# Four raw buffers and a longer lead for a stream of weight blocks in a two-layer encoder kernel

## Chip, cores and metric

The kernel runs on one core of a Trainium2 chip. The metric is the device time of one execution in microseconds (us), the median of several runs.

## What is computed

Two layers, each with an attention mixer and a PEER feed-forward part, on 512 tokens of width 1024, all in float32. The change touches the second part only:

```python
def peer_ffn(x, w_q, sub_keys, u, v):
    ...
        q = (xc @ w_q).reshape(c, PEER_HEADS, 2, PEER_HALF_DIM)
        sc = jnp.einsum('chpd,hpnd->chpn', q, sub_keys, preferred_element_type=jnp.float32)
        top_s, top_i = lax.top_k(sc, kk)
        cand = top_s[:, :, 0, :, None] + top_s[:, :, 1, None, :]
        cand_s, cand_i = lax.top_k(cand.reshape(c, PEER_HEADS, kk * kk), kk)
        ...
        experts = i1 * PEER_N_KEYS + i2
        gates = jax.nn.softmax(cand_s, axis=-1)
        ue = jnp.take(u, experts, axis=0)
        ve = jnp.take(v, experts, axis=0)
        act = jax.nn.gelu(jnp.einsum('chkd,cd->chk', ue, xc), approximate=False)
        return jnp.einsum('chk,chkd->cd', gates.astype(xc.dtype) * act, ve)
```

There are 8 heads, 16 experts per head and token, and 16384 experts of one neuron each. Around it, `x <- LayerNorm(alpha * x + peer)`.

## The kernel before

**Two ways to the same sum.** For the last 384 of the 512 tokens the kernel computes all experts densely: it streams u and v in 128 blocks of 128 experts each (512 KB a block), multiplies, applies gelu and weights the result with gates that are mostly zero. For the first 128 tokens it gathers the rows of u and v that were chosen and forms 128 row products per token on VectorE.

**Stages of a layer.** Projections and attention (to about 385 us in layer 1); the query stage, 16 blocks of `peer_w_q` and the key scores (to about 495); the expert stage, 128 blocks of u; the value stage, 128 blocks of v (1205 to 1725). Layer 2 repeats this some 1730 us later. The expert stage has two parts. In the first, TensorE takes blocks 0 to 88 while VectorE finds the top 16 (32 "units" of 128 tokens and one head; 8 before the gathers and 24 beside them) and forms 96 row products in 12 rounds of two units and eight rows. At its end VectorE and ScalarE turn the scores into gates, and TensorE transposes them before block 89. In the second part one-hot matrices spread the gates over the experts, beside the other blocks.

**A block's way.** A block of the stream passes through these hands, numbered n over the whole layer, with s = n mod 2:

- SyncE's queue asks for it: `st_load` (L378 to L381) waits until the raw buffer is free, then transfers 512 KB into `st_raw[s]`.
- ScalarE rounds it to fp32r: `round_block` (L848 to L852) waits for the landing and until TensorE has used block n-2 (`st_used`), then copies `st_raw` to `st_hi[s]`.
- GpSimd takes the rest: `rest_block` (L605 to L610) writes `st_lo[s] = st_raw[s] - st_hi[s]` and increments `st_l[s]`. For the blocks of v after the first two VectorE does it (`rest_value`, L1379 to L1384), and for query block 0 too.
- TensorE multiplies: `stationary` (L1626 to L1637) waits for `st_h`, makes 16 products with `st_hi` (L1632, L1633), waits for `st_l` and makes 8 with `st_lo` (L1636). In the value stage it is `gather` and `part` (L1715).

The buffers `st_raw`, `st_hi` and `st_lo` have two places each. `st_raw[s]` is free again when `rest_block` has read it, so a block's load waits for the subtraction of the block two before it. The semaphore starts at 1 in each slot:

```python
            def st_load(m, s, src):
                sp.wait_ge(st_l[s], ST_PER // 2 * l + m + 1)
                sp.dma_start(st_raw[:, s], src).then_inc(s_straw[s], 16)
```

**Orders written out by hand.** Every engine executes its list in order. SyncE's queue alternates, in the expert stage, the store of a gelu result (`gelu_store`, L394 to L397: 192 KB from `h_out[s]` to DRAM, after `gelu_done`) and the load of the block of u four further on. In the value stage it alternates a load of v with `gated_load` (L399 to L403), which brings gates and gelu values back. Before the third block of v it waits for the last one-hot product (`g_tok`) and for all gelu stores. ScalarE alternates, for each block b of the expert stage, `gelu(b)` (L877 to L882; it waits for TensorE to finish b and for the store of b-2 to land) and `round_block(b+2)`, with a table load before each pair. After the pair of blocks 86 and 87 (and the rounding of 88 and 89) comes the exponential of the gates (L904), whose sum VectorE takes in L1312; L1316 finishes the gates.

GpSimd alternates subtractions and gathers. `zone` (L634 to L643) fixes the pattern: in `ZONE_R` = 4 rounds of 8 gathers it places `ZONE_BN` = 26 subtractions evenly, after `ZONE_B0` = 6 at the start. A gather (`gather_rows`, L617 to L621; 512 KB into one of 8 places of `u_row`) waits until VectorE has used that place's row of the round before (`u_dot`). VectorE's row products (L1287) stand inside the units, and wait for the gathered row.

**Memory.** The attention part and the PEER part share the same addresses. After `st_raw`, `st_hi`, `st_lo` and `h_out` come `keys` and `pq`, then `scores`, all in the place of the attention's projections, and behind them the top-16 tables and the index tables. In its loop over the four groups of output weights (`k == 2`, L384) the queue waits until nearly all of attention's inputs are read (`v_ready`), then loads `keys` and the first two query blocks, ahead of the last two blocks of the output projection's weights (`w_load`, L359 to L362).

Of the kernel before, what the change touches and what calls it, by code (L numbers as in the profile page):

```python
# [32 lines left out]
P = 128  # L33
L = 2
T = 512
# [47 lines left out]
ZONE_R, ZONE_B0, ZONE_BN = 4, 6, 26  # L83
# [50 lines left out]
def build(nc, a, out):  # L134
# [56 lines left out]
    o_all = att.tile("o_all", [P, TB, JOBS * VD], F32)  # L191
    w_uq = att.tile("w_uq", [P, 2, UQ_W], F32)
# [34 lines left out]
    st_raw = pr.tile("st_raw", [P, 2, DC * P], F32)  # L227
# [4 lines left out]
    keys = pr.tile("keys", [P, QB, NK], F32)  # L232
    pq = pr.tile("pq", [P, 2, T], F32)
# [10 lines left out]
    cab = tk.tile("cab", [P, 2, TOPK], U32)  # L244
    c_all = tk.tile("c_all", [P, UNITS, TOPK], F32)
# [4 lines left out]
    sp_r = Region(tk.end)  # L250
# [31 lines left out]
    assert max(vp.end, sp_r.end) <= ga.start and vp.end <= tk.end and vr.end <= ln_rows_at and tk.end <= u_at  # L282
# [14 lines left out]
    s_straw = [sem(f"s_straw{s}") for s in range(2)]  # L297
# [52 lines left out]
    def _(sp):  # L350
        for dst, src in ((x_tok[:], a["x"]), (ident[:], a["ident"]), (iota[:], a["iota"])):
            sp.dma_start(dst, src).then_inc(s_x, 16)
        with sp.Fori(0, L) as l:
# [24 lines left out]
            def st_load(m, s, src):  # L378

                sp.wait_ge(st_l[s], ST_PER // 2 * l + m + 1)  # L380
                sp.dma_start(st_raw[:, s], src).then_inc(s_straw[s], 16)  # L381

            for k in range(O_G):
                if k == 2:  # L384


                    sp.wait_ge(v_ready, (JOBS - JA) * (l + 1))
                    sp.dma_start(ln_rows[:], a["ln1"][l].partition_broadcast(P)).then_inc(s_ln, 16)
                    sp.dma_start(keys[:], a["peer_keys"][l]).then_inc(s_keys, 16)
                    for s in range(2):  # L390
                        st_load(0, s, a["peer_w_q"][l, s])
# [13 lines left out]
            with sp.Fori(1, QB // 2) as i:  # L405
                for s in range(2):
                    st_load(i, s, a["peer_w_q"][l, 2 * i + s])
# [25 lines left out]
            st_load(1 + (QB + EB) // 2, 0, a["peer_v"][l, 2])  # L433
            for s in range(2):
                gated_load(1, s)
            st_load(1 + (QB + EB) // 2, 1, a["peer_v"][l, 3])
            gated_load(2, 0)
            with sp.Fori(2, EB // 2 - 1) as i:
                for s in range(2):
                    st_load(i + (QB + EB) // 2, s, a["peer_v"][l, 2 * i + s])  # L440
                    gated_load(i + s, 1 - s)
            st_load(EB // 2 - 1 + (QB + EB) // 2, 0, a["peer_v"][l, EB - 2])
            gated_load(EB // 2 - 1, 1)
            st_load(EB // 2 - 1 + (QB + EB) // 2, 1, a["peer_v"][l, EB - 1])
# [7 lines left out]
    def _(pool):  # L452
        step = Steps(pool, pool_step)
        pool.sem_inc(st_l[1], 1)
# [6 lines left out]
        with pool.Fori(0, L) as l:  # L461
# [150 lines left out]
            rest_block(0, 1)  # L612
            with pool.Fori(1, QB // 2 + ZONE_B0 // 2) as m:
                for s in range(2):
                    rest_block(m, s)
# [19 lines left out]
            def zone(z, first=False):  # L635

                done = 0
                for r in range(ZONE_R):
                    for k in round_u(ZONE_R * z + r, r % 2, first and r == 0):
                        while done * ZONE_R * URING < (URING * r + k + 1) * ZONE_BN - ZONE_BN // 2:  # L640
                            rest_block(z * (ZONE_BN // 2) + QB // 2 + (ZONE_B0 + done) // 2, done % 2)
# [1157 lines left out]
```

## Time and profile before

| | us |
|---|---|
| median of 3 runs (lowest, highest) | 3488.45 (3486.89, 3492.88) |
| the profiled execution | 3488.86 |
| its span | 3487.1 |
| TensorE busy | 3273.4 (94%) |
| VectorE busy | 2486.1 (71%) |
| ScalarE busy | 1371.2 (39%) |
| GpSimd busy | 1955.6 (56%) |
| moved by transfers | 765.12 MB, mean 219 GB/s |

The span runs from the first to the last instruction of the profiled execution; its own time is 1.8 us longer. Busy TensorE includes time at a lower granted clock, which the profile gives apart (1.00 is 2.4 GHz). A wait is put down to the instruction that ended it. Waits of engines that are not the last to arrive cost nothing.

### The profile page before, as it was taken

Reading aid. Unit: us, or ns where it says so; the run is one execution under the profiler, and the core shown is the slowest. Engines: PE = TensorE matmul, PEld = TensorE weight load, DVE = VectorE, ACT = ScalarE, POOL = GpSimd, SP = SyncE. Lnnn points to the kernel's source line nnn. Section 1 sums busy time; section 2 is a strip of 40 time slices with the busy share of each in tenths; the row PEclk is TensorE's granted clock in tenths of the full one; section 3 lists DMA queues with packets and bytes.
Section 4 is the critical chain, followed back from the end, with each engine's and each line's share of the span. In section 5 each row is a group of like instructions: output and inputs, shape, how many; then the busy total and the mean of one; then the engine's idle time right before and its main releaser. Section 6 shows DMA issues by size and latency. Waiting matters only on the chain.

```text
span 3487.1 us, 67389 instructions
## 1 busy us (share of the span) xinstructions
PE 3273.4 (94%) x18454; PEld 2957.4 (85%) x18454; DVE 2486.1 (71%) x5419; ACT 1371.2 (39%) x2110; POOL 1955.6 (56%) x1558
## 2 busy tenths in 40 slices
PE   8999899998999899999899998989999998999996
PEld 8888789988999788888798887889999997788885
DVE  1454557887687688888914545578887777889888
ACT  2354234544433333333324542444444333333332
POOL 3434347877654266666544343477775533666665
PEclk9999999999999999999999999999999999999998
DMA  4001138888698599999820011389886986999996
GB/s 161 25 1 61 43 104 280 296 284 277 223 271 254 165 328 342 336 338 336 306 95 24 1 61 49 121 278 312 285 294 223 275 230 199 315 345 337 339 336 229
DMA packets 402487, 765.12 MB, mean 219 GB/s; under 512 B 162400, under 2 KB 261472, under 8 KB 398432
## 3 DMA queue, kind: packets, MB, share of 16 engines
q1 hardware_dynamic: 197088, 462.06, 39.4%
q0 software_dynamic: 73728, 268.47, 21.0%
q10 hardware_dynamic: 131584, 33.56, 4.6%
q8 instruction: 40, 0.66, 0.1%
q14 instruction: 47, 0.39, 0.0%
HBM read 677.98 MB, written 85.98 MB: 219 GB/s over the span
## 4 chain that ended last, share of the span: by engine, by line
PE 57%; issue 20%; POOL 11%; DVE 3%; ACTq 3%; DMA 3%; ACT 2%; POOLq 1%; DVEq 0%; SPq 0%
PE ps L1715 25%; POOL st_lo L608 6%; PE ps L1682 4%; PE ps L1568 3%; POOL u_row L619 3%; PE ps L1632 3%; PE ps L1633 3%; PE ps L1446 3%; PE ps L1636 3%; PE ps L1447 3%; PE ps L1448 3%; PE ps L1545 3%; ACTq L929 2%; PE ps L1553 2%; PE ps L1534 1%
## 5 line engine op out<-in xcount | busy, mean ns | idle before, releaser
L608 POOL TENSOR_TENSOR st_lo<-st_raw,st_hi 128x1024 fp32r<-128x1024 f32 x290 | 697.2, 2405 | 590.8 <-ACT st_hi L852 585.9
L852 ACT CAST st_hi<-st_raw 128x1024 fp32r<-128x1024 f32 x544 | 571.1, 1050 | 908.8 <-PE ps L1715 444.7
L1632 PE MATMUL ps<-t_hi,st_hi 128*128 128x384 f32 (+1 forms) x2304 | 815.9, 354 | 58.0 <-ACT st_hi L852 56.4
L1633 PE MATMUL ps<-t_lo,st_hi 128*128 128x384 f32 (+1 forms) x2304 | 801.4, 348 | 0.0
L712 POOL TENSOR_TENSOR wt_lo<-w_f,wt_hi 128x384 fp32r<-128x384 f32 x256 | 416.8, 1628 | 319.2 <-ACT wt_hi L954 316.1
L1632 PEld LDWEIGHTS ps<-t_hi,st_hi 128*128 128x128 f32 x2304 | 440.3, 191 | 84.0 <-ACT st_hi L852 68.1
L1636 PE MATMUL ps<-t_hi,st_lo 128*128 128x384 f32 (+1 forms) x2304 | 468.4, 345 | 2.2 <-POOL st_lo L608 2.1
L1633 PEld LDWEIGHTS ps<-t_lo,st_hi 128*128 128x128 f32 x2304 | 440.5, 191 | 10.0
L1636 PEld LDWEIGHTS ps<-t_hi,st_lo 128*128 128x128 f32 x2304 | 412.7, 189 | 16.3 <-POOL st_lo L608 5.1
L1715 PE MATMUL ps<-st_hi,wt_hi 128*128 128x512 f32 x1536 | 391.0, 390 | 9.9 <-ACT wt_hi L954 9.9
L1715 PE MATMUL ps<-st_lo,wt_hi 128*128 128x512 f32 x1536 | 389.8, 389 | 0.0
L1715 PE MATMUL ps<-st_hi,wt_lo 128*128 128x512 f32 x1536 | 389.7, 389 | 0.0
L1382 DVE TENSOR_TENSOR st_lo<-st_raw,st_hi 128x1024 fp32r<-128x1024 f32 x252 | 315.0, 1250 | 79.3 <-ACT st_hi L852 78.0
L1715 PEld LDWEIGHTS ps<-st_hi,wt_hi 128*128 128x128 f32 x1536 | 287.5, 188 | 73.2 <-ACT st_hi L852 10.3
L1715 PEld LDWEIGHTS ps<-st_lo,wt_hi 128*128 128x128 f32 x1536 | 288.3, 188 | 60.0
L1715 PEld LDWEIGHTS ps<-st_hi,wt_lo 128*128 128x128 f32 x1536 | 288.3, 188 | 59.9
L1391 DVE SCALAR_TENSOR_TENSOR ps<-v_row,w_sp,ps 128x1024 f32<-128x1024 f32 x256 | 326.9, 1277 | 0.8
L1374 DVE TENSOR_TENSOR w_f<-g_in,h_in 128x256 f32<-128x256 f32 x256 | 252.2, 985 | 61.9 <-DMA h_in<-gelu_d 48.0
L1287 DVE CUSTOM_DVE_ANT_0 u_row<-ps,u_row 128x1024 f32<-128x1024 f32 x192 | 233.1, 1214 | 84.8 <-DMA u_row<-in_peer_ur,idx_u 83.6
L882 ACT ACTIVATE h_out<-ps 128x384 f32<-128x384 f32 x256 | 125.2, 489 | 425.0 <-PE ps L1636 371.7
L619 POOL DMA_INDIRECT v_row<-in_peer_v,idx_v x256 | 257.5, 1006 | 44.5 <-issue 18.4
L1338 DVE TENSOR_SCALAR oh<-ps,i_t,g_t 128x128 f32<-128x128 f32 x768 | 260.5, 400 | 0.0
(194 smaller groups left out, 5091.7 us busy)
## 6 DMA issues: line engine op xcount, KB each, us to landing
st_raw<-in_peer_u SPq DMA_DIRECT2D x256, 512.0 KB
st_raw<-in_peer_v SPq DMA_DIRECT2D x256, 512.0 KB
gelu_d<-h_out SPq DMA_DIRECT2D x256, 192.0 KB
h_in<-gelu_d SPq DMA_DIRECT2D x256, 192.0 KB
gates_d<-g_stage ACTq DMA_DIRECT2D x32, 1024.0 KB
g_in<-gates_d SPq DMA_DIRECT2D x256, 128.0 KB
w_raw<-in_w_in SPq DMA_DIRECT2D x16, 1168.0 KB, 5.2
st_raw<-in_peer_w_q SPq DMA_DIRECT2D x32, 512.0 KB
```

Of the source, the lines that this page charges most:

```text
L608: nc.gpsimd.tensor_tensor(st_lo[:, s].rearrange("p c f -> p (c f)"), st_raw[:, s], st_hi[:, s].rearrange("p c f -> p (c f)").bitcast(F32), ...
L619: nc.gpsimd.indirect_dma_start(out=dst, out_offset=None, in_=table, in_offset=bass.IndirectOffsetOnAxis(ap=number, axis=0)).then_inc(lande ...
L712: nc.gpsimd.tensor_tensor(wt_lo[:, s], w_f[:, s], wt_hi[:, s].bitcast(F32), ALU.subtract).then_inc(wt_l, 1)
L852: nc.scalar.copy(st_hi[:, s].rearrange("p c f -> p (c f)"), st_raw[:, s]).then_inc(st_h, 1)
L1338: last = nc.vector.tensor_scalar(oh_1[:, GRP * r + k], iota_ps, i_t[:, 0, ds(t0 + k, 1)], g_t[:, ds(t0 + k, 1)], ALU.is_equal, ALU.mult)
L1374: nc.vector.tensor_tensor(w_f[:, s, 0:T_D], g_in[:, s], h_in[:, s, 0:T_D], ALU.mult)
L1382: nc.vector.tensor_tensor(st_lo[:, s].rearrange("p c f -> p (c f)"), st_raw[:, s], st_hi[:, s].rearrange("p c f -> p (c f)").bitcast(F32), ...
L1391: nc.vector.scalar_tensor_tensor(out=acc, in0=v_row[:, r], scalar=w_sp[:, ds(b, 1)], in1=acc, op0=ALU.mult, op1=ALU.add).then_inc(v_acc, 1)
L1632: nc.tensor.matmul(dst, st_hi[:, s, c], t_hi[:, c, rows], start=c == 0, stop=False)
L1633: nc.tensor.matmul(dst, st_hi[:, s, c], t_lo[:, c, rows], start=False, stop=False)
L1636: last = nc.tensor.matmul(dst, st_lo[:, s, c], t_hi[:, c, rows], start=False, stop=c == DC - 1)
L1715: last = nc.tensor.matmul(ps[:, 2 * d + half], w[:, s, d * P:(d + 1) * P], v[:, half * 512:(half + 1) * 512], start=False, stop=True, skip ...
```

## The change

`st_raw` gets four places instead of two (`RAW = 4`), each with its own landing semaphore; `st_hi` and `st_lo` keep two. The semaphores `st_l` start at 2 (`PRIME`), so that a load waits for the subtraction of the block four before it. In the expert stage the load after the gelu store of block b is that of block b+6 instead of b+4; the first four blocks of v are asked for there. In the value stage loads of v stand two blocks further ahead of the gate products. Four query blocks instead of two are asked for before the last weights of the output projection. `keys` and `pq` move to the place of the attention's tables, and the index tables behind the buffers of the value stage. The zones of GpSimd become 6 rounds with 40 subtractions (`ZONE_R`, `ZONE_BN`). Loops over blocks run over four places at once or are unrolled.

```diff
-ZONE_R, ZONE_B0, ZONE_BN = 4, 6, 26
+ZONE_R, ZONE_B0, ZONE_BN = 6, 6, 40
+VALUE_BYTES = 4 * (3 * TN + 2 * OH_T * P + UDOTS * D + 2 * T_D + 8 * TN)
+RAW = 4
...
+    tables_at = att.end
...
-    st_raw = pr.tile("st_raw", [P, 2, DC * P], F32)
+    st_raw = pr.tile("st_raw", [P, RAW, DC * P], F32)
...
-    keys = pr.tile("keys", [P, QB, NK], F32)
-    pq = pr.tile("pq", [P, 2, T], F32)
+    qk = Region(tables_at)
+    keys = qk.tile("keys", [P, QB, NK], F32)
+    pq = qk.tile("pq", [P, 2, T], F32)
...
-    sp_r = Region(tk.end)
+    sp_r = Region(shared + VALUE_BYTES)
...
-            def st_load(m, s, src):
+            def st_load(m, r, src):
-                sp.wait_ge(st_l[s], ST_PER // 2 * l + m + 1)
-                sp.dma_start(st_raw[:, s], src).then_inc(s_straw[s], 16)
+                sp.wait_ge(st_l[r % 2], ST_PER // 2 * l + m + 1)
+                sp.dma_start(st_raw[:, r], src).then_inc(s_straw[r], 16)
...
-                    for s in range(2):
-                        st_load(0, s, a["peer_w_q"][l, s])
+                    for r in range(RAW):
+                        st_load(r // 2, r, a["peer_w_q"][l, r])
...
-            for b in range(4):
-                st_load(QB // 2 + b // 2, b % 2, a["peer_u"][l, b])
-            with sp.Fori(0, EB // 2 - 2) as i:
-                for s in range(2):
-                    gelu_store(i, s)
-                    st_load(i + QB // 2 + 2, s, a["peer_u"][l, 2 * i + 4 + s])
-            for s in range(2):
-                gelu_store(EB // 2 - 2, s)
-                st_load((QB + EB) // 2, s, a["peer_v"][l, s])
+            for b in range(RAW + 2):
+                st_load(QB // 2 + b // 2, b % RAW, a["peer_u"][l, b])
+            with sp.Fori(0, EB // RAW - 2) as i:
+                for r in range(RAW):
+                    gelu_store(2 * i + r // 2, r % 2)
+                    st_load(2 * i + QB // 2 + RAW // 2 + 1 + r // 2, (r + 2) % RAW, a["peer_u"][l, RAW * i + RAW + 2 + r])
+            for b in range(EB - 2 * RAW, EB - 2):
+                gelu_store(b // 2, b % 2)
+                n = b + RAW + 2
+                st_load((QB + n) // 2, n % RAW, a["peer_u"][l, n] if n < EB else a["peer_v"][l, n - EB])
...
-            st_load(1 + (QB + EB) // 2, 0, a["peer_v"][l, 2])
+            st_load((QB + EB + RAW) // 2, 0, a["peer_v"][l, RAW])
             for s in range(2):
                 gated_load(1, s)
-            st_load(1 + (QB + EB) // 2, 1, a["peer_v"][l, 3])
+            st_load((QB + EB + RAW) // 2, 1, a["peer_v"][l, RAW + 1])
             gated_load(2, 0)
-            with sp.Fori(2, EB // 2 - 1) as i:
-                for s in range(2):
-                    st_load(i + (QB + EB) // 2, s, a["peer_v"][l, 2 * i + s])
-                    gated_load(i + s, 1 - s)
...
+            with sp.Fori(1, EB // RAW - 1) as i:
+                for k in range(RAW):
+                    st_load(2 * i + (QB + EB) // 2 + 1 + k // 2, (k + 2) % RAW, a["peer_v"][l, RAW * i + 2 + k])
+                    gated_load(2 * i + (k + 1) // 2, (k + 1) % 2)
...
-        pool.sem_inc(st_l[1], 1)
+        pool.sem_inc(st_l[1], PRIME)
...
-            def rest_block(m, s):
+            def rest_block(m, r):
+                s = r % 2
                 pool.wait_ge(st_h, ST_PER * l + 2 * m + s + 1)
-                nc.gpsimd.tensor_tensor(st_lo[:, s].rearrange("p c f -> p (c f)"), st_raw[:, s],
+                nc.gpsimd.tensor_tensor(st_lo[:, s].rearrange("p c f -> p (c f)"), st_raw[:, r],
...
-            def round_block(m, s):
+            def round_block(i, r):
-                act.wait_ge(s_straw[s], (ST_PER // 2 * l + m + 1) * 16)
-                act.wait_ge(st_used, ST_PER * l + 2 * m + s + 1)
-                nc.scalar.copy(st_hi[:, s].rearrange("p c f -> p (c f)"), st_raw[:, s]).then_inc(st_h, 1)
+                act.wait_ge(s_straw[r], (ST_PER // RAW * l + i + 1) * 16)
+                act.wait_ge(st_used, ST_PER * l + RAW * i + r + 1)
+                nc.scalar.copy(st_hi[:, r % 2].rearrange("p c f -> p (c f)"), st_raw[:, r]).then_inc(st_h, 1)
...
-        dve.sem_inc(st_l[0], 1)
+        dve.sem_inc(st_l[0], PRIME)
...
-                pe.wait_ge(st_l[s], ST_PER // 2 * l + m + 1 + 1)
+                pe.wait_ge(st_l[s], ST_PER // 2 * l + m + 1 + PRIME)
```

## Rows read from the trace of the kernel before

**Rows 1.** The page, section 2: the transfer engines' busy tenths in 40 slices.

```profile
DMA  4001138888698599999820011389886986999996
```

**Rows 2.** Table by stage: stretch, length, busy time of PE, PEld, DVE, ACT, POOL, clock, DMA.

```profile
500.00:920.00 420.00, 387.25 (x2110) 381.48 (x2109) 315.53 (x1004) 194.43 (x265) 304.99 (x197) 0.97 0.81 270
2237.00:2645.00 408.00, 381.76 (x2116) 373.29 (x2115) 312.71 (x1001) 196.63 (x266) 305.79 (x197) 0.99 0.83 279
...
1250.00:1725.00 475.00, 475.00 (x2097) 393.32 (x2096) 423.55 (x468) 172.34 (x235) 314.42 (x264) 1.00 0.95 336
```

**Rows 3.** Waits (us, times, longest): two of the whole run, one of 500 to 920.

```profile
ACT st_hi L852 <- DMA st_raw<-in_peer_u: 237.4, 122, 6.1
PE ps L1632 <- ACT st_hi L852: 56.4, 31, 3.5
...
PE ps L1632 <- ACT st_hi L852: 32.1, 15, 2.9
```

**Rows 4.** Waits of SyncE's queue and GpSimd, 500 to 920; of ScalarE, 915 to 1180.

```profile
SPq L381 <- POOL st_lo L608: 296.2, 88, 7.4
...
POOL st_lo L608 <- ACT st_hi L852: 89.9, 37, 5.6
...
ACT st_hi L852 <- DMA st_raw<-in_peer_u: 0.2, 1, 0.2
```

**Rows 5.** Timeline, 698 to 708: start, length, engine, line, what, idle time before.

```profile
698.35 0.33 SPq L381 DMA_DIRECT2D st_raw<-in_peer_u  x1
...
699.25 2.44 POOL L608 TENSOR_TENSOR st_lo<-st_raw,st_hi 128x1024 fp32r<-128x1024 f32 x1
...
706.79 1.04 ACT L852 CAST st_hi<-st_raw 128x1024 fp32r<-128x1024 f32 x1 [5.44 <-DMA st_raw<-in_peer_u]
```

**Rows 6.** Timeline of ScalarE: gelus of blocks 0 and 2, and block 0 of layer 2.

```profile
501.89 0.49 ACT L882 ACTIVATE h_out<-ps 128x384 f32<-128x384 f32 x1 [1.22 <-PE ps L1636]
...
510.31 0.49 ACT L882 ACTIVATE h_out<-ps 128x384 f32<-128x384 f32 x1 [1.42 <-PE ps L1636]
...
2238.60 0.49 ACT L882 ACTIVATE h_out<-ps 128x384 f32<-128x384 f32 x1 [1.22 <-PE ps L1636]
```

**Rows 7.** Row products to gates: timelines of both layers; VectorE's waits, 500:920 and 2237:2645.

```profile
524.91 1.22 DVE L1287 CUSTOM_DVE_ANT_0 u_row<-ps,u_row 128x1024 f32<-128x1024 f32 x1 [13.88 <-DMA u_row<-in_peer_ur,idx_u]
...
901.25 0.16 DVE L1300 TENSOR_TENSOR dots<-dot,ps 128x8 f32 x1 [0.42 <-DVE i_all L1260]
...
919.56 1.28 ACT L904 ACT_TABLE_LOAD   x1
...
921.52 0.69 DVE L1312 TENSOR_REDUCE z_all<-e_all 128x32 f32<-128x512 f32 x1 [17.87 <-ACT e_all L904]
...
922.62 0.69 DVE L1316 TENSOR_TENSOR e_all<-e_all,z_all 128x512 f32<-128x512 f32 x1
...
2627.05 0.16 DVE L1300 TENSOR_TENSOR dots<-dot,ps 128x8 f32 x1 [0.43 <-DVE i_all L1260]
...
2645.30 0.69 DVE L1312 TENSOR_REDUCE z_all<-e_all 128x32 f32<-128x512 f32 x1 [16.58 <-ACT e_all L904]
...
DVE u_row L1287 <- DMA u_row<-in_peer_ur,idx_u: 46.6, 35, 13.9
...
DVE u_row L1287 <- DMA u_row<-in_peer_ur,idx_u: 37.0, 17, 13.8
```

**Rows 8.** Timelines: the last gather of the part, and a gelu held by a store.

```profile
889.19 0.96 POOL L619 DMA_INDIRECT u_row<-in_peer_ur,idx_u  x1 [0.16 <-issue]
...
720.86 0.49 ACT L882 ACTIVATE h_out<-ps 128x384 f32<-128x384 f32 x1 [1.85 <-DMA gelu_d<-h_out]
```

**Rows 9.** Timeline of SyncE's queue, two issues; TensorE's wait at L1715, whole run.

```profile
328.20 0.34 SPq L362 DMA_DIRECT2D w_raw<-in_w_o  x1
...
1203.53 0.35 SPq L381 DMA_DIRECT2D st_raw<-in_peer_v  x1
...
PE ps L1715 <- ACT wt_hi L954: 9.9, 8, 2.0
```

More of the change, by code:

```diff
@@ L296, in build @@
     s_wraw = [sem(f"s_wraw{s}") for s in range(2)]
-    s_straw = [sem(f"s_straw{s}") for s in range(2)]
+    s_straw = [sem(f"s_straw{r}") for r in range(RAW)]
     s_gh = [sem(f"s_gh{s}") for s in range(2)]
@@ L650, in _ @@
             b_body = 2 * (PRE + 1)
-            with pool.Fori(QB // 2 + (ZONE_B0 + U_ROUNDS // ZONE_R * ZONE_BN) // 2, (QB + b_body) // 2) as m:
-                for s in range(2):
-                    rest_block(m, s)
+            rest_pairs(QB // 2 + (ZONE_B0 + U_ROUNDS // ZONE_R * ZONE_BN) // 2, (QB + b_body) // 2)
             def numbers_b(t, half):
@@ L689, in _ @@
             body_blocks(B_ROUNDS - 1, 1, more=False)
-            with pool.Fori((QB + b_body) // 2 + 2 * B_ROUNDS, (QB + EB) // 2 + 1) as m:
-                for s in range(2):
-                    rest_block(m, s)
+            rest_pairs((QB + b_body) // 2 + 2 * B_ROUNDS, (QB + EB) // 2 + 1)
             v_rows_all = a["peer_v"].rearrange("l b p d -> (l b p) d")
@@ L894, in load_table @@
                 nc.scalar.activation(warm[:], eps[:], ACT.Gelu).then_inc(warm_done, 1)
-            round_block(QB // 2, 1)
-            with act.Fori(0, PRE) as i:
-                load_table(i)
-                for s in range(2):
-                    gelu(i, s)
-                    round_block(i + QB // 2 + 1, s)
+            round_number(QB + 1)
+            assert PRE % 2 == 0
+            with act.Fori(0, PRE // 2) as i:
+                for f in range(2):
+                    load_table(2 * i + f)
+                    for s in range(2):
+                        gelu(2 * i + f, s)
+                        round_block(i + QB // RAW + (f + 1) // 2, (2 * f + 2 + s) % RAW)
             act.wait_ge(gate_sub, l + 1)
@@ L906, in _ @@
             gelu(PRE, 0)
[L907 removed]
+            round_number(2 * PRE + QB + 2)
             for k in range(3):
@@ L937, in stage_body @@
                     gelu(first + b // 2, b % 2)
-                    round_block(first + b // 2 + QB // 2 + 1, b % 2)
-            for w in range(WIN):
-                with act.Fori(0, BODIES - (w == WIN - 1)) as q:
-                    stage_body(w, w % 2, q, 0 < w < WIN - 1, 2 if w * BODIES < B_ROUNDS else 1)
+                    ahead = QB + 2 * PRE + 4 + b
+                    if pairs == 2:
+                        round_block(body + ahead // RAW, ahead % RAW)
+                    else:
+                        round_number(ahead + 2 * (body + B_ROUNDS))
+            for w in range(WIN):
+                if w * BODIES < B_ROUNDS:
+                    with act.Fori(0, BODIES) as q:
+                        stage_body(w, w % 2, q, 0 < w, 2)
+                else:
+                    for q in range(BODIES - (w == WIN - 1)):
+                        stage_body(w, w % 2, q, w < WIN - 1, 1)
             for g in range(GROUPS):
@@ L957, in _ @@
                 round_gated(b, b)
-            with act.Fori(0, EB // 2 - 1) as i:
-                for s in range(2):
-                    round_block(i + (QB + EB) // 2 + 1, s)
-                    round_gated(2 * i + s + 2, s)
+            with act.Fori(0, EB // RAW - 1) as i:
+                for r in range(RAW):
+                    round_block(i + (QB + EB) // RAW + (r + 2) // RAW, (r + 2) % RAW)
+                    round_gated(RAW * i + r + 2, r % 2)
+            for s in range(2):
+                round_number(QB + 2 * EB - 2 + s)
+                round_gated(EB - 2 + s, s)
             deviation(1)
```

64 lines of the change are left out of this document (38 added, 26 removed).

## The prediction

> **What bounds the kernel now.** The views stand in the order in which I read them. The page: TensorE is busy 94% of the span (the table above), and the transfer engines' digit, 0 to 3 in the attention and query stages, is 8 in slices 7 to 10 and 9 in slices 15 to 19, and so again in layer 2 [rows 1]. The table by stage separates these two stretches [rows 2]. In the value stage (1250 to 1725) TensorE has no gap although the transfer engines stand at 0.95 and 336 GB/s. In the part of the expert stage that also gathers rows (500 to 920) it is idle 32.8 of 420 us, at a granted clock of 0.97, in layer 2 26.2 of 408 us at 0.99, while the transfer engines have more room (0.81 and 0.83).
>
> The waits name the cause [rows 3]. Over the whole run TensorE waits 56.4 us for ScalarE's rounding of a streamed block (L852), 32.1 of them in the gather part of layer 1. The other 24.3 are layer 2's; none is left for the query or value stages. ScalarE in turn waits 237.4 us for blocks of u to land, up to 6.1 us at once. The queue that asks for them stands 296.2 of 420 us before L381, until GpSimd's subtraction (L608) has freed the raw buffer [rows 4]. One late block shows the loop [rows 5]. Its load is asked for at 698.35; rounding starts at 706.79, 8.4 us later and 5.44 us after ScalarE was free for it. The other buffer came free only with the subtraction that ended at 701.7. So with two buffers one turn is landing 8.4, rounding 1.0, subtraction 2.4: 11.8 us and the queueing between, where TensorE uses two blocks in 8.42 us (the gelus at 501.89 and 510.31 are two blocks apart) [rows 6]. When landing is quick the loop holds, with gathers beside it it doesn't.
>
> What this costs: the gates are ready at 923.3 and 2647.1 (VectorE's last instruction on them ends there; in layer 2 I add the same 1.8 us to the start of the sum) [rows 7]. TensorE without a gap would be through block 88 at 501.9 + 87 x 4.21 + 4.2 = 872.4, in layer 2 at 2238.6 + 366.3 + 4.2 = 2609.1. So 50.9 and 38.0 us lie in this part, more than the waits alone: a clock of 0.97 over 420 us is 12.6 us on top of 32.1, and 0.99 over 408 us is 4.1 on top of 24.3; the clock falls after such gaps.
>
> **The change, part by part.** *Four raw buffers.* A load still waits for a subtraction, that of the block four back. It is asked for at the same event as now (the subtraction of block b+2), but for b+6 instead of b+4, so it has two blocks, 8.4 us, more to land. The latest was 6.1 us late. All these waits of the gather part go. Bytes stay, and the number in flight hardly grows, as one load is asked for per block.
>
> The row shows 8.4 us for 512 KB beside gathers and stores [rows 5]. By the Trainium skill ("SBUF — State Buffer", the DMA setup-cost knee), a transfer takes 2 us plus its bytes over 436 GB/s, an estimate of 3.2 us here. By that figure two buffers would be enough and this sum would be nought; the measurement decides.
>
> *Does the traffic fit?* 96 gathers of 0.524 MB and, beside them, some 83 blocks of 0.524 MB with their 0.197 MB of gelu stored are 110 MB. From some 6 us before the first row product at 524.9 [rows 7] to 870 that is 314 GB/s, a share near 0.9; the value stage moves 336 at 0.95 without a gap [rows 2].
>
> *What is late next: VectorE,* which has 24 units with 96 row products there (12 rounds). It takes from 524.9 to 901.4, and waits 46.6 us for rows, 13.9 of them the first wait, before 524.9 [rows 7]. The rest is 343.8 us, 28.7 a round, where the 6.67 blocks that the new zone puts beside a round take TensorE 28.1. The later waits, 32.7 us (37.0 - 13.8 = 23.2 in layer 2), come from gathers that GpSimd issues late, since it stands 89.9 us before subtractions until the block is rounded [rows 4]. They go. I keep 5 us a layer for rows that fuller transfer engines bring late. The pass ends at 901.4 - 32.7 + 5 = 873.7 and at 2627.2 - 23.2 + 5 = 2609.0. Today VectorE then stands 17.87 and 16.58 us before the gates' sum [rows 7], because ScalarE is in order behind 88 blocks; after, ScalarE is there first, and what stays is 2.2 us (two instructions of VectorE), 2.0 (table load and exponential, 919.56 to 921.52) and 1.8: 6.0. Gates at 879.7 and 2615.0: **43.6 and 32.1 us** gained, 7.3 and 5.9 under what TensorE alone would allow.
>
> *Zones of 6 rounds and 40 blocks instead of 4 and 26.* Per round GpSimd then has 6.67 subtractions of 2.4 us and 8 gathers of 1.0 with some 0.2 between, and 1.2 for the numbers: 27 us at most, under 28.1 [rows 5, 8]. The last gather moves behind two more blocks (85 done instead of 83). At full pace block 84 is rounded 1.5 us after the gelu of 82, at 501.9 + 82 x 4.21 + 1.5 = 848.6, and subtracted at 851; 12.2 us later, as today (889.19 to 901.4) [rows 7, 8], VectorE could be done, at 863. Nought, covered by the pass itself, which ends at 873.7; uncovered, 8.4 us a layer.
>
> *The turn to the value stage.* Today block v2 is asked for at 1203.53, after the last one-hot product [rows 9]; after, v0 to v3 lie there by then. In the whole run TensorE waits 9.9 us for rounded gate products (L954), all of it at these two turns, and ScalarE gets to L954 late because it stands before blocks of v in its order. Bounds: 0, where the gelu values' own transfers hold it, and 9.9; I take **5**, the middle, as nothing in the row separates them. Later in the value stage TensorE has no gap to give.
>
> *Two more query blocks ahead, keys and queries in another place.* Two issues more and 1 MB at 308 on SP's queue, ahead of the output weights' loads, which wait until 328.2 anyway [rows 9]: 20 us cover some 4 us. Nothing else reads the new place then; nought. *One-hot part:* ScalarE waited 0.2 us for blocks of u there [rows 4], nothing to gain. *Unrolled loops, two priming increments larger:* a few register instructions beside over 100 us of idle time of ScalarE and of GpSimd in the gather part [rows 2]; nought, 1 us either way.
>
> Sum: 43.6 + 32.1 + 5 = 80.7 us off the profiled execution's 3488.9 (span 3487.1; 0.4 over the median of the runs): **3408 us**. The bounds together give 50.9 + 38.0 + 9.9 = 98.8, hence 3390.
>
> **Rivals.** *A, the transfers take half of it back (0.20).* The gelu store becomes the late one. It shares SP's queue with the loads' waits, and its slot is wanted again 8.4 us after it was filled. One of these waits stands at 720.86, 1.85 us [rows 8]. TensorE feels it from 2.7 us on (a block of 4.2 less 1.5 for gelu and rounding), and at full pace there is less slack. Against it: none has reached TensorE yet. With half of 75.7 and of 5 lost it is 3448 us, from 3425 to 3465.
>
> *B, it doesn't do what it says (0.04).* Loads are late because the transfer engines are full; then the lead is used up within a few blocks and every block waits as before. For it: the digit 8. Against it: SP stood 296 us with nothing it was allowed to ask for. Time: 3482 to 3492, say 3487.
>
> *C, slower (0.04): gathers starve.* Loads never pause any more, and rows land later. VectorE's 32.7 and 23.2 us double, and the zone puts the last gather 8.4 us later. The pass ends 41.1 and 31.6 us later, less the 17.87 and 16.58 that it stands anyway: 23.2 + 15.0 = 38.2 us slower, 3527 us. It decides from the point where the pass ends over 18 us later than now (17 in layer 2). Against it: one load per block remains, and the value stage runs gathers and loads at a higher rate without a gap.
> By the Trainium skill ("DMA: Bandwidth & Descriptors", queues, rings and completion order), each transfer engine takes turns between the queue rows that have work, a packet each, so a load row that is never empty would slow the gathers; no row here shows the turns.
>
> **Numbers.** Forecast 0.72, A 0.20, B 0.04, C 0.04. The forecast's own range is 3390 to 3427: the bounds on one side, and on the other a quarter of the sum lost to rows and stores that land late. For 8 in 10 I take 3393 to 3442, halfway into A. A measurement of this kernel tells about 0.2%, 7 us, from no change. Faster by more: 0.72 + 0.20 + 0.01 = 0.93; within: 0.03; slower: 0.04.
>
> **What would show it.** Right: TensorE's waits on L852 in the gather part near nought and its clock at 1.0 there; no wait of ScalarE for u; GpSimd's 89.9 us down to a third; gates near 880, with TensorE standing some 6 us before them; a transfer share above 0.9. Wrong: ScalarE's waits for the gelu store reaching TensorE (A), the old waits still there (B), VectorE waiting over 3 us a round (C), or a one-hot or value stage that has grown.

## The result and the profile after

The changed kernel takes 3399.97 us (median of 4 runs, 3396.17 to 3401.21) beside 3490.25 us of the kernel before in the same rounds: a ratio of 0.974, interval 0.9723 to 0.9757. The profiled execution took 3400.1 us with a span of 3398.3, against 3488.9 and 3487.1. The forecast was 3408 us: the kernel gained 8 us more than forecast, within the range of 3390 to 3427.

The table by stage of the changed kernel, with the columns of [rows 2]: the two gather parts, the one-hot part of layer 1, the value stage.

```profile
503.00:873.00 370.00, 370.00 (x2105) 369.81 (x2104) 309.73 (x995) 160.30 (x242) 304.98 (x196) 1.00 0.91 307
2195.00:2564.00 369.00, 368.16 (x2085) 366.23 (x2084) 308.46 (x985) 158.19 (x239) 302.89 (x196) 1.00 0.90 306
875.00:1156.00 281.00, 261.40 (x1718) 256.53 (x1719) 223.83 (x560) 108.92 (x192) 128.67 (x82) 0.98 0.76 225
1200.00:1670.00 470.00, 470.00 (x2076) 389.20 (x2075) 422.75 (x461) 168.26 (x231) 306.05 (x259) 1.00 0.95 336
```

TensorE has no gap in the gather part of layer 1 and a granted clock of 1.00, where it was idle 32.8 of 420 us at 0.97 [rows 2]; in layer 2 it is idle 0.8 of 369 us, before 26.2 of 408. The transfer engines, at 0.81 before, are now at 0.91. The next fence has the waits of the changed kernel, the first four of the whole run, the others of 500 to 875 alone (us, times, longest), to be read beside [rows 3], [rows 4] and [rows 7].

```profile
PE ps L1664 <- ACT st_hi L865: 0.2, 1, 0.2
ACT h_out L899 <- DMA gelu_d<-h_out: 124.5, 42, 5.6
ACT g_stage L938 <- issue: 72.5, 16, 4.9
PE ps L1714 <- ACT g_stage L938: 30.9, 24, 4.6
...
ACT h_out L899 <- DMA gelu_d<-h_out: 47.8, 17, 4.4
POOL st_lo L617 <- ACT st_hi L865: 43.1, 45, 5.2
DVE u_row L1318 <- DMA u_row<-in_peer_ur,idx_u: 17.0, 4, 13.8
...
SPq L387 <- POOL st_lo L617: 250.5, 89, 7.1
```

TensorE's 56.4 us for rounded blocks are 0.2, and ScalarE's 237.4 us for blocks of u have no row left at all. A new wait has come: ScalarE waits 124.5 us for the gelu stores, before 12.3. Then the end of the gather part, from the timelines of VectorE and TensorE (start, length, engine, line, what, idle time before and its releaser):

```profile
869.15 0.16 DVE L1331 TENSOR_TENSOR dots<-dot,ps 128x8 f32 x1 [0.43 <-DVE i_all L1291]
...
873.65 0.69 DVE L1343 TENSOR_REDUCE z_all<-e_all 128x32 f32<-128x512 f32 x1 [2.85 <-ACT e_all L924]
...
874.75 0.69 DVE L1347 TENSOR_TENSOR e_all<-e_all,z_all 128x512 f32<-128x512 f32 x1
...
875.50 0.88 PE L1704 MATMUL ps<-ident,i_all 128*128 128x128 f32 x6 [1.08 <-DVE e_all L1347]
```

The pass over the rows ends at 869.3 (901.4 before), the gates are there at 875.44 (923.3), and TensorE stands (is idle, waiting) 1.08 us for them. The two engines have met: both bound this part now, within a microsecond.

Cut at the same events, the span fell by 88.8 us, thus: gather part 49.1 in layer 1 and 33.5 in layer 2; one-hot parts 1.3 and 1.2; value stages 1.6 and 7.3; end 0.2; lost were 1.2 at the start, before the first gelu, and 4.3 in the second layer's attention.

### The profile page after: what moved, and what is told of

Same layout as the page of the kernel before. It is cut to its first block, busy times and chain, and to the rows that moved or that the text cites. A ratio compares the mean times of both kernels' runs of the same rounds, so it can differ in the third digit from the quotient of the medians.

```text
span 3398.3 us, 66597 instructions
## 1 busy us (share of the span) xinstructions
PE 3252.3 (96%) x18452; PEld 2950.3 (87%) x18454; DVE 2491.6 (73%) x5419; ACT 1298.3 (38%) x2066; POOL 1949.6 (57%) x1558
## 4 chain that ended last, share of the span: by engine, by line
PE 78%; issue 8%; POOL 4%; DVE 4%; ACTq 2%; DMA 1%; ACT 1%; DVEq 0%; POOLq 0%; SPq 0%
PE ps L1747 30%; PE ps L1664 8%; PE ps L1668 8%; PE ps L1665 8%; PE ps L1714 4%; PE ps L1600 4%; PE ps L1478 3%; PE ps L1577 3%; PE ps L1479 3%; PE ps L1480 3%; POOL st_lo L617 3%; PE ps L1585 2%; ACTq L949 2%; PE ps L1566 1%; POOL u_row L636 1%
## 5 line engine op out<-in xcount | busy, mean ns | idle before, releaser
L1664 PE MATMUL ps<-t_hi,st_hi 128*128 128x384 f32 (+1 forms) x2304 | 804.5, 349 | 1.6 <-DVE t_lo L1020 1.3
L1668 PEld LDWEIGHTS ps<-t_hi,st_lo 128*128 128x128 f32 x2304 | 411.3, 188 | 12.9 <-POOL st_lo L617 1.7
L1405 DVE TENSOR_TENSOR w_f<-g_in,h_in 128x256 f32<-128x256 f32 x256 | 259.6, 1014 | 58.3 <-DMA h_in<-gelu_d 47.7
```

The costliest lines, as they stand in the source:

```text
L1405: nc.vector.tensor_tensor(w_f[:, s, 0:T_D], g_in[:, s], h_in[:, s, 0:T_D], ALU.mult)
L1664: nc.tensor.matmul(dst, st_hi[:, s, c], t_hi[:, c, rows], start=c == 0, stop=False)
L1668: last = nc.tensor.matmul(dst, st_lo[:, s, c], t_hi[:, c, rows], start=False, stop=c == DC - 1)
```

## The experiments

**Only the zones.** The kernel before with GpSimd's larger zones, and two raw buffers as before.

```diff
-ZONE_R, ZONE_B0, ZONE_BN = 4, 6, 26
+ZONE_R, ZONE_B0, ZONE_BN = 6, 6, 40
```

> The kernel before with the zones of 6 rounds and 40 subtractions alone, two raw buffers. Theory (the raw buffers are what gained): 3482 to 3494 us, same as before; TensorE's waits on the rounding stay at 50 to 60 us over the run, ScalarE's waits for u near 237 us. Rival (the zones freed GpSimd and VectorE, and the buffers only followed): 3400 to 3450 us, with TensorE's waits down by half or more.

Measured: 3487.41 us, ratio to the kernel before 0.9986 (0.9966 to 1.0007). Its waits in the whole run:

```profile
ACT st_hi L852 <- DMA st_raw<-in_peer_u: 237.7, 120, 5.8
PE ps L1632 <- ACT st_hi L852: 58.2, 33, 3.6
```

Both are those of [rows 3]: the zones do nothing for the loads. **Only the buffers** is the other half: the changed kernel with the old zones of 4 rounds and 26 blocks (the zone loop is written out, since 26 is no multiple of four buffers).

```diff
-ZONE_R, ZONE_B0, ZONE_BN = 6, 6, 40
+ZONE_R, ZONE_B0, ZONE_BN = 4, 6, 26
```

> The changed kernel with the old zones (4 rounds, 26 subtractions, unrolled). Theory: 3396 to 3406 us, no wait of TensorE on a rounded block; GpSimd issues its gathers a little earlier against TensorE's blocks (6.5 for 6.67 a round) and may wait for VectorE. Rival (VectorE at 28.4 us a round is slower than 6.5 blocks at 27.4 us, so GpSimd falls behind VectorE and its subtractions come late): 10 to 24 us slower than the changed kernel, 3410 to 3424 us, with waits of TensorE at its last eight products.

Measured: 3399.57 us, ratio 0.9732 (0.969 to 0.9775), the changed kernel's time. The gain needs nothing of the zones. This run still has all the other parts of the change (the lead, the query blocks ahead, the new places), but the gather parts, where the blocks of u used to be late, hold 82.6 of the 88.8 us.

**A shorter lead with the same four buffers.** Two kernels ask for block b+4 and b+5 where the changed one asks for b+6.

```diff
+LEAD = 4
...
-            for b in range(RAW + 2):
+            for b in range(LEAD):
...
-                    st_load(2 * i + QB // 2 + RAW // 2 + 1 + r // 2, (r + 2) % RAW, a["peer_u"][l, RAW * i + RAW + 2 + r])
+                    st_load(2 * i + (QB + LEAD + r) // 2, (r + LEAD) % RAW, a["peer_u"][l, RAW * i + LEAD + r])
```

> The changed kernel with a lead of four blocks instead of six in the expert stage (four raw buffers stay, after the gelu store of block b the load of b+4). Without the wait for the subtraction of b+2 the load is asked for about 0.7 us after gelu(b) instead of 4.5 us, so it has 7.7 us until ScalarE wants it and 10.4 us until TensorE does, against landings of up to 8.4 us. Theory (what counted is that the request no longer waits for a subtraction just made): 3396 to 3408 us, ScalarE waits for u again (20 to 100 us over the run), TensorE under 3 us. Rival (the two extra blocks of lead are needed): half of the stalls come back, 3430 to 3460 us.

> The same with a lead of five. The load of b+5 waits for the subtraction of b+1, which ended before gelu(b), so SyncE's queue stands free when a gelu store is due. Theory: 3394 to 3404 us, no waits for u, and ScalarE's waits for the gelu store (124.5 us over the run in the changed kernel, 12.3 before) fall under 40 us, since the store is no longer queued behind a load's wait. Rival (those waits come from fuller transfer engines, not from the queue's order): they stay at 80 us and more. The time is the same in both, as no such wait reached TensorE.

Measured: 3427.71 us (ratio 0.9818, 0.9775 to 0.9861) with a lead of four, 3414.83 (0.9766, 0.9721 to 0.9812) with five. In the gather part a lead of four is all that is needed: 372.5 us in both layers (after: 372.4 and 375.0); ScalarE waits 2.8 us for blocks in the whole run, and its waits for the gelu store are gone, with either lead. What grew is the one-hot part: 299.7 us in layer 1 and 295.0 in layer 2 with a lead of four, 292.9 and 290.2 with five, in place of 281.3 and 281.4. Its work is a loop of twelve "bodies" a layer, and eight of them store finished gates. The timelines of the kernel with lead four show one of these, ScalarE first, then TensorE:

```profile
931.21 0.46 ACTq L952 DMA_DIRECT2D gates_d<-g_stage  x1
...
931.87 5.56 ACTq L952 DMA_DIRECT2D gates_d<-g_stage  x1
937.81 1.07 ACT L941 COPY g_stage<-ps 128x512 f32 x2 [5.95 <-issue]
...
938.45 2.60 PE L1717 MATMUL ps<-oh,oh 128*128 128x128 f32 x16 [2.15 <-ACT g_stage L941]
```

ScalarE issues the two stores of finished gates itself, 1 MB each and back to back. The second issue holds it 5.56 us, in the changed kernel 4.40, and for so long no gate copy is made; TensorE stands 2.15 us for one, in the changed kernel 0.98. What follows the stand is in the table by 2 us of the same kernel:

```profile
936.00:938.00 2.00, 0.30 (x2) 0.00 (x0) 0.42 (x2) 0.19 (x1) 0.00 (x0) 1.00 1.21 293
938.00:940.00 2.00, 1.55 (x13) 1.55 (x14) 0.14 (x1) 2.00 (x4) 0.00 (x0) 0.94 1.01 301
940.00:942.00 2.00, 2.00 (x9) 2.00 (x9) 2.00 (x6) 1.28 (x3) 1.71 (x1) 0.50 1.21 291
942.00:944.00 2.00, 2.00 (x10) 2.00 (x9) 2.00 (x6) 0.00 (x0) 1.62 (x2) 0.70 1.21 313
944.00:946.00 2.00, 2.00 (x14) 2.00 (x13) 1.00 (x3) 0.00 (x0) 0.00 (x0) 1.00 1.03 357
```

The granted clock falls to 0.50 (the lower level, 1.2 GHz) after the stand. After the changed kernel's stand of 0.98 us it stays at 1.00. This body takes 28.0 us in place of 25.1. So my expectation missed because a longer issue on another engine, which nothing in the gather part hinted at, was paid for twice: in the stand and in the clock. The clock did not fall each time: of the twelve stands of 2.0 to 3.1 us in both layers, eight were followed by stretches of 3.4 or 6.8 us at 0.50 (not, for one, that of 2.10 us that ended at 1022.40). "After each such stand", as an expectation below has it, is too much.

**Are the loads late for traffic or for GpSimd's order?** The kernel before, two buffers and all, but the gathers beside the key blocks carry 64 of 1024 columns. VectorE multiplies those over and over, so the dots and the output are not the reference's; GpSimd issues the same gathers in the same places.

```diff
-                    gather_rows(u_row[:, k], idx_u[:, half, k:k + 1], a["peer_ur"], s_urow[k])
+                    gather_rows(u_row[:, k, 0:64], idx_u[:, half, k:k + 1], a["peer_un"], s_urow[k])
```

> This is the kernel BEFORE (two raw buffers, a load asked for 3.9 us before ScalarE wants it) with one thing taken away: the six row gathers of a zone carry 64 of 1024 columns from a table of its own, and DVE's product reads those 64 columns over and over (the same element count, written to a space of its own), so the dots are wrong and the traffic beside the weight loads is about 3 MB a token tile less. GpSimd still issues every gather in the same place. Theory (the loads were late because they shared the DMA engines with the gathers, and the request was made too late for that): a load lands inside 3.9 us, ScalarE's waits for the loads (237.7 us in the kernel before) fall under 60 us, TensorE's for st_hi (88.5 us) under 20, and the time is 3400 to 3420 although there are only two buffers. Rival (the loads were late because GpSimd's own gather instructions delayed the subtraction that frees a buffer, whatever the transfers weigh): the waits stay, 3475 to 3490.

Measured: 3408.41 us (3398.07 to 3418.77), ratio 0.9745 (0.9705 to 0.9786). Its gather part in the table by stage, and ScalarE's wait in the whole run:

```profile
503.00:873.00 370.00, 370.00 (x2104) 370.00 (x2104) 309.52 (x995) 191.92 (x263) 305.13 (x196) 1.00 0.59 179
...
ACT st_hi L854 <- DMA st_raw<-in_peer_u: 11.1, 21, 1.2
```

With 179 GB/s in place of 270 the old two buffers feed TensorE without a gap. The loads were late because the transfers beside them made them land late, and not because of what GpSimd had to issue. The deeper buffers do not take that lateness away, they give it room: in the changed kernel a block of the gather parts still lands 5.6 (layer 1) and 6.1 us (layer 2) after its request, by the median, and two buffers left 3.9 in layer 1.

**The value turn.** The changed kernel with its third and fourth value block asked for only after the last one-hot product.

```diff
+            for n in range(2, RAW):
+                st_load((QB + EB + n) // 2, n, a["peer_v"][l, n])
             st_load((QB + EB + RAW) // 2, 0, a["peer_v"][l, RAW])
```

> The changed kernel with one part undone: the third and fourth value block of a layer are asked for only after the last one-hot product, not with the last key blocks. The two first stay early. This prices the value turn that I put at 5 us for both layers. Theory (the early third and fourth value block are what spares the turn): 5 to 9 us more than the changed kernel, so 3405 to 3409, all of it between the first value product and the fourth block. Rival (the turn is bound by something else, the gates or ScalarE's rounding): no change within 1.5 us.

Measured: 3412.98 us (ratio 0.976, 0.9728 to 0.9792), 13.0 more, above both expectations; the two value stages are 14.8 us longer than the changed kernel's. TensorE stands 6.56 us from 1166.97 in layer 1 (0.51 in the changed kernel) and 4.45 in layer 2 (nought). ScalarE's timeline tells why:

```profile
1163.43 1.05 ACT L868 CAST st_hi<-st_raw 128x1024 fp32r<-128x1024 f32 x1 [4.56 <-DMA st_raw<-in_peer_v]
1172.84 0.51 ACT L985 CAST wt_hi<-w_f 128x384 fp32r<-128x384 f32 x1 [8.36 <-DVE w_f L1409]
```

The long wait is not for a block but for the gated product, whose gates and gelus are now asked for behind three loads of 512 KB on the same queue. So this run bounds the price of late value blocks from above and does not isolate it: it is no pure undoing, as the kernel before asked for one block there, not three. What the early third and fourth block gain by themselves is not shown.

**A version that beats both.** The 30.9 us that TensorE stands for gate copies are there before (33.9) and after. Two kernels take them up. One issues the gates' stores from SyncE's queue, the first a block before the body, the second half a body later:

```diff
-                    for part in range(2):
-                        n0 = q * 2 * n_q + part * n_q
-                        act.dma_start(gates_d[ds(n0, n_q), :, ds(w * WIN_T - WIN_T, WIN_T)].rearrange("n p t -> p n t"),
-                                      g_stage[:, 1 - sw, ds(n0, n_q)]).then_inc(s_gst[1 - sw], 16)
...
+                for key in place.get(b, []):
+                    gates_store(*key)
```

> The changed kernel with the gates' stores of the one-hot part (two to a body, 32 in both layers) issued from SyncE's queue and not from ScalarE's, where the second of a pair holds ScalarE for 4.4 us and TensorE then stands for a gate copy: 0.9 us in six bodies and 4.1 to 4.6 us in two of a layer, 14.1 us in a layer, with a granted clock of 0.83 and 0.91 around the two long ones. This looks for a version better than both. Theory (ScalarE's issue time is what TensorE pays): TensorE's gaps for gate copies go, the one-hot part falls from 281.4 to 262 to 268 us, and the time is 3360 to 3375. Rival (the store holds whichever queue issues it, and on SyncE's it delays the request of the next block and the gelu stores by 4.4 us twice a body): new waits of ScalarE for the weight loads, one-hot part 275 to 290, 3390 to 3415.

Measured: 3358.31 us (3355.53 to 3361.72), ratio to the kernel before 0.9601 (0.957 to 0.9632). The table by stage of its one-hot part, 264 us with 0.99 of the clock where the changed kernel has 281 with 0.98:

```profile
876.00:1140.00 264.00, 256.27 (x1712) 253.32 (x1711) 223.66 (x559) 107.81 (x191) 128.53 (x81) 0.99 0.83 239
```

and SyncE's queue around one of the stores:

```profile
934.09 0.40 SPq L422 DMA_DIRECT2D gates_d<-g_stage  x1
936.17 4.31 SPq L403 DMA_DIRECT2D gelu_d<-h_out  x1
```

The store itself takes its queue 0.40 us. The issue behind it takes 4.31: the time has moved to whoever issues next on that queue, where TensorE hardly feels it. Its stands for gate copies are 7.0 us in the whole run, where they were 30.9. That made a test worth while in which both stores stay on ScalarE, but half a body apart:

```diff
                 if store:
                     act.wait_ge(g_ev, TN // GRP * l + WIN_T // GRP * w + RING)
-                    for part in range(2):
...
+                    gates_store(0)
...
                     gelu(first + b // 2, b % 2)
+                    if store and b == pairs - 1:
+                        gates_store(1)
```

> The changed kernel with the two gates' stores of a body left on ScalarE's queue, but no longer back to back: the first at the body's start, as now, the second after half of the body's key blocks. In the changed kernel the first issue of a pair takes 0.4 us and the second 4.4; on SyncE's queue (e7) each of them took 0.4 us, and the gelu store issued 2 us behind one took 4.3. Theory (what holds a queue is an issue made within some microseconds behind a 1 MB gates' store on the same queue, not the store's own issue): each store takes 0.4 to 0.6 us of ScalarE, the one-hot part is 262 to 268 us as in e7, and the time 3355 to 3370. Rival (a gates' store costs ScalarE 4 us by itself, and e7 gained because SyncE's queue takes it better): every body has one stand still, of the first or of the second store, and the time is 3385 to 3405.

Measured: 3355.96 us (3351.17 to 3359.21), ratio 0.9605 (0.9577 to 0.9633), the same time as from SyncE's queue. ScalarE's timeline and two of its waits in the whole run (the last is TensorE's):

```profile
930.45 0.45 ACTq L948 DMA_DIRECT2D gates_d<-g_stage  x1
...
941.77 0.41 ACTq L948 DMA_DIRECT2D gates_d<-g_stage  x1
...
ACT g_stage L938 <- issue: 0.2, 1, 0.2
...
PE ps L1719 <- ACT g_stage L938: 4.3, 12, 0.5
```

Each store now costs ScalarE 0.4 us, and TensorE's stand is 4.3 us in place of 30.9. It was the second issue close behind a large one that cost, not the queue it stood on. Nor is it a hold on both queues: in the changed kernel SyncE issues a load during each of ScalarE's 16 long issues, and each takes 0.33 us. By the Trainium skill ("DMA: Bandwidth & Descriptors", issuing engines are not separate DMA queues), issuing from several engines only saves the sequencer's time, "which is usually small relative to the DMA itself". The transfers here land alike from either queue (medians of 8.7 us from SyncE's, 7.5 from ScalarE's spread apart), which agrees; the sequencer's time is what decided 34 to 38 us of this kernel, which the "usually small" does not let one expect. By stages: both one-hot parts together take 562.7 us in the changed kernel, 528.8 with the stores on SyncE's queue and 524.4 spread apart on ScalarE's, so 34 and 38 us; the rest of the 42 to 44 lies in stretches that the stores don't touch, most of it in the attention of layer 2, which differs as much between two profiles of one kernel (below).

**Lead four again, with that stand gone.** The kernel with a lead of four and the stores from SyncE's queue.

> Four raw buffers with a lead of four blocks (as in e3, 3427.7 us), and the gates' stores issued from SyncE's queue (as in e7, 3358.3 us with a lead of six). In e3 ScalarE's issue of the second store of a pair lasted 5.6 us in place of 4.4, TensorE stood 2.1 us in place of 0.9 in six bodies of a layer, and its granted clock was 0.50 for some 4 us after each such stand. Theory (that issue time was all that a lead of four cost; as a lead for the weight loads four blocks do with four buffers): 3355 to 3365, one-hot parts of 265 to 270 us. Rival (with four blocks of lead the loads of the one-hot part are late by themselves, beside the gates' stores): 3370 to 3410, with waits of ScalarE for st_raw in the one-hot part.

Measured: 3356.58 us, ratio 0.9605 (0.9589 to 0.9621), as with a lead of six; the one-hot parts take 261.9 us each. ScalarE waits 4.2 us for blocks of u in the whole run. So the issue on ScalarE was all that the shorter lead cost, and of the change's two parts, four buffers and six blocks of lead, a lead of four would do for the loads.

**And on two buffers.** The kernel before, with only the gates' stores on SyncE's queue.

> The kernel BEFORE with its two raw buffers, and only the gates' stores of the one-hot part moved to SyncE's queue. It asks whether that gain (41.7 us on the changed kernel) needs the deeper buffers. Theory A (the two changes touch different stages and add): 3490 less 38 to 44, so 3443 to 3455. Theory B (with only 3.9 us between the request and ScalarE's need, each store ahead of a request on SyncE's queue, and its 256 KB on the transfer engines, make a load late in the one-hot part too): 3460 to 3490, with new waits of ScalarE for st_raw there.

Measured: 3452.51 us, ratio 0.9884 (0.9862 to 0.9905): 41.5 us less than before, where it was 41.7 on the changed kernel. The two gains add. That they agree to 0.2 us is luck: the median of the kernel before itself was 3490.3 to 3496.6 us in the rounds of these runs. Its gather parts (411.9 and 416.2 us) are still long, its one-hot parts short (266.1 and 263.7): 35.4 us less than before, where they were 33.9 less on the changed kernel. (A store carries 1024 KB by the page, not the 256 of the expectation.)

**The changed kernel once more,** for a second profile.

> The changed kernel once more, word for word, for a second profile. The stretch from the last value product of layer 1 to layer 2's first gelu took 511.9 us in its first profile against 507.7 in the kernel before, and 506.7 to 511.9 in the experiments so far. If those 4 us are scatter of the clock's grants between executions, the stretch comes out anywhere in 506 to 512 and most likely below 511; if they belong to the changed placement of keys and query staging, it is 511 to 513 again.

Measured: 3396.4 us; the stretch took 508.0 us, where the first profile had 511.9 and the kernel before 507.7. Over the thirteen profiles of this study it lies between 506.2 and 512.1, with no order in buffers, lead or stores: with the old placement of keys and queries 507.7, 511.8 (zones only), 507.6 (thin gathers) and 511.2 (two buffers, stores from SyncE), with the new one 506.2 to 512.1. The 4.3 us lost there are scatter between executions.

## Why the prediction was right

*The cause.* Loads late by their landing, asked for too late by two buffers: shown, by the thin gathers from one side and by four buffers, with the old zones and with a lead of four, from the other. The price, 8.4 us more to land for a load that was up to 6.1 late, was enough. The lead of four shows that the longer lead was not needed: with four buffers the request for b+4 waits for the subtraction of block b, no longer for that of b+2, and that alone is early enough (in the gather part of layer 1 a median of 7.5 us from the request until ScalarE is free to round the block, where two buffers gave 3.9 and the changed kernel gives 12.9). I had taken lead and buffers for one thing.

*Gather part: 43.6 and 32.1 us forecast, 49.1 and 33.5 measured.* My table of the traffic (314 GB/s, share near 0.9) came out at 307 and 0.91. VectorE's pass ends at 869.3 for a forecast 873.7: it began 1.1 us later and took 343.3 us, where I had 343.8 and 5 of allowance for late rows. Rows were late by 3.2 us after the first wait in layer 1 (17.0 less 13.8), 4.9 in layer 2, so the allowance was well sized. The other term was not: of the 343.8 us that I took for VectorE's own time, some 3.7 went with the waits. They were not other waits: beside busy time and waits for rows the pass has 39.3 us before and 39.4 after. It is busy time that fell, from 304.2 to 300.7 us, for the same 971 instructions, whose lengths add up to 344.7 and 344.5 us. So they overlap more where fewer of them wait, and a wait for a row cost a little more than its row in the list. The steps from pass to gates, 6.0 forecast, took 6.1 and 6.9. That TensorE would stand some 6 us before the gates was wrong, it is 1.08: the pass came sooner and TensorE's own blocks ended at 874.4, not 872.4, 1.2 of it the later start.

*GpSimd's 89.9 us down to a third:* 43.1, half, and it did no harm. *Zones: nought,* right, shown by the first two runs. *Query blocks ahead, keys' place: nought;* no run has them alone, but nothing speaks against it: the first gelu starts at 501.9 to 503.6 us in the four profiles without them and at 502.5 to 504.6 in the nine with them, and layer 2's attention is told above. *The value turn: 5 us forecast,* 8.9 measured over both layers. TensorE's stands for rounded gate products, 9.9 us before [rows 9], lost 7.4 of them; 1.5 us of layer 2 I can't place. The chain of the kernel before shows how far they reach (start, length, what, instructions):

```profile
1249.17 473.60 PE ps L1715 x2088
...
3043.10 408.29 PE ps L1715 x1800
```

These are the chain's last rows of each layer, TensorE without a gap to the end of the stage. In layer 2 it begins at 3043.10, 113 us into the stage, behind five stands of 0.5 to 1.6 us; after, the same rows begin at 1165.73 and 2848.43, the latter the first product of all. I had put all 9.9 us "at these two turns" and let the value stage have no gap behind them, from a row of layer 1 that began at 1250, 0.8 us after its last stand, and took layer 2 to be the same. And the middle of the bounds was the wrong end; 2.5 of the 9.9 us stayed. The 8.9 are themselves one pair of profiles: both value stages together take 1047.1 to 1060.8 us in the four profiles with two buffers and 1045.0 to 1046.6 in the eight with four and early value blocks, so the gain is anything from 1 to 15 us. *One-hot part: nought,* 2.4 measured, through somewhat shorter stands for gate copies (in layer 1 before 5.15 and 5.08 at the longest, after 4.56 and 4.15).

*Rival A* had its mechanism right and its price wrong. The gelu store did become the late one, 124.5 us in the whole run, 5.6 at the longest. That gelu came at 2491.22, 7.1 us after the one before it at a pace of 4.2, so 2.9 late, and the next three made up for it. I had put TensorE's threshold at 2.7, and so it was: TensorE stands 0.19 us at 2492.70 for the block rounded behind that gelu, the one wait of 0.2 us in the fence above. The 5.6 us count from ScalarE's last work, and 2.7 of them would have gone in waiting for TensorE in any case: a wait of the list is not a delay of the same size. Two things stand behind the late store. In SyncE's queue it stands behind a load that waits for a subtraction (this one was issued 2.2 us after its gelu), and it lands late (this one took 8.45 us, where the median of the gather parts is 5.9; the store behind the wait at 862.91 was issued at once and took 8.4). With a lead of four or five, where no store is issued more than 0.2 us after its gelu, the waits have gone from the list altogether. The kernel before, with less traffic beside its stores, waited only 12.3 us though its stores stood longer in the queue (a median of 2.0 us from gelu to issue, 0.5 after). So the order of the queue has a part in these waits and the fuller transfer engines may have another; how they divide is open, as the landings of the runs with lead four and five can't be read.

*B and C* did not come: every load had its lead until the end, and rows cost 3.2 and 4.9 us, not 32.7 and 23.2 twice over.

So the total is right by its parts, with errors of 5.5 (gather part of layer 1), 1.4 (layer 2), 3.9 (value turn) and 2.4 us (one-hot parts) by which it gained more than forecast, and on the other side 5.5 us of start and attention that the execution profiled happened to have. Without these the gain would have been 13 us over the forecast, still within the range; that the total comes out as near as 8 is in part luck. What the study adds is what the prediction left out: the one-hot part, which I passed over with a row that spoke of loads alone (0.2 us), held another 34 to 38 us.

## What to carry to other kernels

A streamed operand needs its request as far ahead as its landing takes beside the other traffic of the same stage, not alone; read that from the stretch between the issue's row and the consumer's. Give the ring as many buffers as it takes that the lead, and not a free buffer, sets the request, and then check what stands behind the loads in the same queue. And look at how long an engine that also computes is held by its own DMA issues: two large stores back to back held ScalarE 4.4 us, the same two half a stage apart 0.4 each.

## What the runs showed of the hardware that I had not expected

A DMA issue close behind one of these 1 MB stores on the same queue takes 3.5 to 7.2 us in place of 0.4. It was seen on ScalarE's queue, 0.7 us behind the first store (4.40, and 5.56 with a lead of four), and on SyncE's, 2.1 us behind (4.31 in the rows above; 3.54 to 7.18 over the 24 such issues of that run). The later the next issue comes, the less it is held: 1.0 to 1.2 us where it comes 4.5 us behind the store, 0.5 to 2.0 at some 5.2 us (the kernel with lead four and stores from SyncE), 0.33 at 7.3 to 7.5, and 0.41 half a body, some 11 us, later. Back to back the second store also lands later: 12.2 to 17.9 us after its issue in the changed kernel, the first 7.3 to 7.8. Why the issue was longer with a lead of four is open. There the load of a block goes out at 931.61, between the two stores of the pair, and with a lead of six at 934.10; that was not tried by itself.

A stand of TensorE of 2.15 us was followed by a granted clock of 0.50 and 0.70 for some 4 us, one of the eight out of twelve stands of 2.0 to 3.1 us that the lower clock followed; the changed kernel's stands of 0.82 to 1.12 us in the same places were followed by none below 1.00. In the kernel with lead four the slower clock cost as much as the longer stands themselves, and more: the table by stage has its one-hot part of layer 1 first, then that of the changed kernel.

```profile
875.00:1175.00 300.00, 271.86 (x1719) 266.76 (x1719) 224.32 (x561) 109.97 (x194) 128.75 (x82) 0.94 0.72 213
...
875.00:1157.00 282.00, 261.62 (x1719) 256.75 (x1721) 224.43 (x561) 109.81 (x194) 128.99 (x83) 0.98 0.76 226
```

For the same 1719 instructions TensorE is busy 10.2 us more, and idle 7.8 us more (28.1 less 20.4).
